# Sums of squares of the dilated heads from a rounded and a remaining part, in a large one-core transformer kernel

## The reference, cut to what matters

```python
qkv = (h @ w_in).reshape(bsz, seq, A_N_GROUPS, 3, A_HEADS, A_HEAD_DIM)   # 3 groups, q/k/v, 16 heads of 64
for g, (window, dilation) in enumerate(A_GROUPS):
    q = rope(rms_norm(qkv[:, :, g, 0], q_gain[g]), positions)
    k = rope(rms_norm(qkv[:, :, g, 1], k_gain[g]), positions)
    v = qkv[:, :, g, 2]
    o, lse = dilated_window_attention(q, k, v, window, dilation)
# rms_norm: x * rsqrt(mean(x*x over the 64 of a head) + 1e-6) * gain
```

## Time and profile before

| | us |
|---|---|
| median of 3 runs | 3809.71 (3798.45 to 3812.93) |
| the profiled execution, its own time | 3802.57 |
| its span | 3800.8 |
| dilated stage, first stretch (from 1966 to 2101 us) | 135 |
| dilated stage, second stretch (2101 to 2640 us) | 539 |
| TensorE busy over the span | 3484.3 (92%) |
| VectorE, ScalarE, GpSimd busy | 1575.9, 1416.8, 1190.1 |

### The profile page before, as it was taken

One profiled execution on the slowest core, in us unless ns is written; L12 is line 12 of the kernel. 1 busy time (PEld: TensorE's weight loads), 2 busy tenths in 40 slices (PEclk: granted clock), 3 DMA queues, 4 the chain that ended last, 5 costly groups with the idle time before them and its releaser, 6 DMA issues.

```text
span 3800.8 us, 43950 instructions
## 1 busy us (share of the span) xinstructions
PE 3484.3 (92%) x17208; PEld 2664.7 (70%) x17208; DVE 1575.9 (41%) x2226; ACT 1416.8 (37%) x1742; POOL 1190.1 (31%) x555
## 2 busy tenths in 40 slices
PE   7999897799959999999638999999899999899999
PEld 4975586578736667666427777777688887678887
DVE  4136525630166666666542332333432132443212
ACT  4225432252235555555133344433432223243221
POOL 2410022634302333333024333322144443334443
PEclk9999998999979999999769999999999999999999
DMA  5322110012227999999623222222032221013222
GB/s 214 102 70 80 66 67 23 1 67 99 89 103 265 348 347 354 366 366 356 268 70 98 69 68 72 73 62 95 23 110 92 99 89 67 23 67 110 93 97 78
DMA packets 94477, 494.51 MB, mean 130 GB/s; under 512 B 21646, under 2 KB 21902, under 8 KB 43760
## 3 DMA queue, kind: packets, MB, share of 16 engines
q1 hardware_dynamic: 74496, 452.75, 33.5%
q0 software_dynamic: 19824, 39.54, 2.9%
HBM read 470.18 MB, written 40.89 MB: 134 GB/s over the span
## 4 chain that ended last, share of the span: by engine, by line
PE 44%; DVE 2%; ACT 2%; issue 1%; POOL 1%; POOLq 0%; DMA 0%; ACTq 0%; DVEq 0%
PE ps L272 10%; PE ps L274 10%; PE ps L273 10%; PE ps L2219 2%; PE ps L2196 2%; PE ps L2174 1%; PE ps L2186 1%; PE ps L2207 1%; PE ps L2175 1%; PE ps L2176 1%; PE ps L2198 1%; PE ps L2848 0%; PE ps L280 0%; PE ps L279 0%; PE ps L278 0%
## 5 line engine op out<-in xcount | busy, mean ns | idle before, releaser
L272 PE MATMUL ps<-arena_r,arena_r 128*128 128x512 f32 x2080 | 842.6, 405 | 39.8 <-POOL ring_r L263 25.0
L273 PE MATMUL ps<-arena_r,arena_r 128*128 128x512 f32 x2080 | 816.0, 392 | 0.0
L263 POOL TENSOR_TENSOR ring_r<-ring,arena_r 128x2048 fp32r<-128x2048 f32 x100 | 466.1, 4662 | 870.8 <-ACT arena_r L259 870.8
L259 ACT ACTIVATE arena_r<-ring 128x2048 fp32r<-128x2048 f32 x166 | 316.6, 1909 | 562.2 <-PE ps L274 408.2
L272 PEld LDWEIGHTS ps<-arena_r,arena_r 128*128 128x128 f32 x2080 | 394.1, 189 | 144.5 <-issue 52.6
L273 PEld LDWEIGHTS ps<-arena_r,arena_r 128*128 128x128 f32 x2080 | 394.7, 190 | 88.5 <-issue 10.6
L263 POOL TENSOR_TENSOR arena_r<-ring,arena_r 128x2048 fp32r<-128x2048 f32 x66 | 304.2, 4609 | 414.2 <-ACT arena_r L259 414.1
L274 PE MATMUL ps<-arena_r,arena_r 128*128 128x512 f32 x1056 | 410.8, 389 | 0.0
L274 PE MATMUL ps<-arena_r,ring_r 128*128 128x512 f32 x1024 | 404.9, 395 | 0.0
L1949 DVE TENSOR_TENSOR arena_r<-arena,arena_r 128x2048 fp32r<-128x2048 f32 x132 | 301.9, 2288 | 168.5 <-ACT arena_r L1907 168.3
L1907 ACT ACTIVATE arena_r<-arena 128x2048 fp32r<-128x2048 f32 x132 | 250.5, 1910 | 125.9 <-DMA arena<-we_gu 102.6
(11 more groups left out here) (392 smaller groups left out, 6017.8 us busy)
## 6 DMA issues: line engine op xcount, KB each, us to landing
ring<-wstream SPq DMA_DIRECT2D x193, 1024.0 KB, 4.9
arena<-we_gu SPq DMA_DIRECT2D x132, 1024.0 KB, 8.2
arena<-we_down SPq DMA_DIRECT2D x66, 1024.0 KB, 7.5
arena<-ys SPq DMA_DIRECT2D x32, 512.0 KB, 8.5
arena<-arena SPq DMA_DIRECT2D x192, 64.0 KB, 2.0
arena<-arena SPq DMA_DIRECT2D x32, 128.0 KB, 4.5
arena<-x_t SPq DMA_DIRECT2D x1, 2048.0 KB, 15.1
h<-arena SPq DMA_DIRECT2D x1, 2048.0 KB, 6.6
```

The lines of the kernel that those rows point to most:

```text
L259: act.activation(whalf(c, 0), ring[:, c % NSLOT, :], ACT.Copy).then_inc(sem("chunk_hi"), 1)
L263: pool.tensor_tensor(whalf(c, 1), ring[:, c % NSLOT, :], whalf(c, 0).bitcast(F32), ALU.subtract).then_inc(sem("chunk_lo"), 1)
L272: pe.matmul(out, hi, rhs[0], start=start, stop=False)
L273: pe.matmul(out, hi, rhs[1], start=False, stop=False)
```

## The change

The square is made twice by ScalarE: DSQ in float32 as before, and DSQ_HI in the rounded type. VectorE subtracts the two into DSQ_LO (`square_low`, one TENSOR_TENSOR with both inputs in SBUF). The sum is then made by two products of rounded numbers, of a rounded copy of `pair` with DSQ_HI and DSQ_LO. The copy of the raw projection comes after the squares and has two buffers, so that it waits for the norm before last only. The sums stand ahead of the fifth eighth of the next half, no longer behind the first.

```diff
+        DRAWS = (DRAW, view(R + 32768, T))
+        DSQ_HI, DSQ_LO, PAIR = rounded(R + 33792, T), rounded(R + 34304, T), rounded(R + 33280, P)
...
                 def between(eighth):
-                    if eighth == 1 and before is not None:
-                        pair_sums(before, h - 1)
                     if eighth == 2 and aside is not None:
                         aside()
+                    if eighth == 4 and before is not None:
+                        pair_sums(before, h - 1)
...
             def pair_sums(n, h):
-                pe.wait_ge(sem("dil_evac"), h + 1)
+                pe.wait_ge(sem("dil_sq_lo"), n + 1)
                 if n >= 1:
                     pe.wait_ge(sem("dil_ln"), n)
-                pe.matmul(bank(7), C["pair"], DSQ, start=True, stop=True).then_inc(sem("dil_ss"), 1)
+                pe.matmul(bank(7), PAIR, DSQ_HI, start=True, stop=False)
+                pe.matmul(bank(7), PAIR, DSQ_LO, start=False, stop=True).then_inc(sem("dil_ss"), 1)
...
+                    if n >= 2:
+                        act.wait_ge(sem("dil_qn"), n - 1)
                     if n >= 1:
-                        act.wait_ge(sem("dil_qn"), n)
                         act.wait_ge(sem("dil_ss"), n)
-                    act.activation(DRAW, bank(5 + h % 2), ACT.Copy)
-                    act.activation(DSQ, bank(5 + h % 2), ACT.Square).then_inc(sem("dil_evac"), 1)
+                    act.activation(DSQ, bank(5 + h % 2), ACT.Square)
+                    act.activation(DSQ_HI, bank(5 + h % 2), ACT.Square).then_inc(sem("dil_sq"), 1)
+                    act.activation(DRAWS[n % 2], bank(5 + h % 2), ACT.Copy).then_inc(sem("dil_evac"), 1)
...
+            act.activation(PAIR, C["pair"], ACT.Copy)
...
-                dve.scalar_tensor_tensor(DQN, DRAW, v(("a_q_norm", "a_k_norm")[s], g, 1), DRS,
+                dve.scalar_tensor_tensor(DQN, DRAWS[n % 2], v(("a_q_norm", "a_k_norm")[s], g, 1), DRS,
                                          ALU.mult, ALU.mult).then_inc(sem("dil_qn"), 1)
+
+            def square_low(h):
+                n = dil_norm(h)
+                dve.wait_ge(sem("dil_sq"), n + 1)
+                dve.tensor_tensor(DSQ_LO, DSQ, DSQ_HI.bitcast(F32), ALU.subtract).then_inc(sem("dil_sq_lo"), 1)
...
-            def step(h):
+            def step(h, with_square=True):
+                if with_square and dil_norm(h - 1) is not None:
+                    square_low(h - 1)
                 if h >= 2 and dil_norm(h - 2) is not None:
                     rotated(h - 2)
...
             for u in range(LAST):
+                first = dil_share(u)[0]
+                if dil_norm(first - 1) is not None:
+                    square_low(first - 1)
                 masked_max(u)
...
                 for h in dil_share(u):
-                    step(h)
+                    step(h, h != first)
```

More of the change, by code:

```diff
@@ L115 @@
     "ff0_value", "ff0_silu", "ff0_hid_hi", "ff0_hid_lo", "ff0_down", "ff0_down_sum",
-    "ff1_value", "ff1_silu", "ff1_hid_hi", "ff1_hid_lo", "ff1_down", "ff1_down_sum",
+    "ff1_value", "ff1_silu", "ff1_hid_hi", "ff1_hid_lo", "ff1_down", "ff1_down_sum", "dil_sq", "dil_sq_lo",
 )
```

## The result

| | before | changed |
|---|---|---|
| median, 7 runs each | 3809.71 us (3797.44 to 3817.74) | 3783.42 us (3777.85 to 3792.88) |
| profiled execution, own time | 3802.57 | 3779.68 |
| stage: first product to first scores | 141.0 | 131.6 |
| first scores to last product of a half | 543.5 | 527.8 |

The ratio of the changed kernel to the one before is 0.9939, with a 95% interval of 0.9921 to 0.9957. The kernel is faster by 0.6%, 26 us between the medians and 23 us between the two profiled executions.

A forecast was written before the change was run, and what follows sets the result against it. TensorE was taken as the bound, so only time off its stream or waits counts. Savings of 7.5 and 15.2 us gave 3779.9 from the profile, 3787.0 from the median; forecast 3783 us, its own range 3774 to 3792, overall 3762 to 3802.

The forecast's parts named there:

- The sum: Whole kernel: 7.5 and 15.2 us saved in the two stretches, 22.7 us off the profiled 3802.6, giving 3779.9.
- the clock: First stretch: granted clock falls to half three times behind waits, costing 1.7 us each; no change counted, 5 us either way.
- Cost of the split sums, 0.45 us: TensorE: both rounded products of a sum take 0.45 us with no float32 switch; 0.97 if they behave like the old ones.
- Waits behind odd halves, 1.27 us, nine: TensorE ahead of sums: VectorE's subtraction is ready 4.0 us after an odd half, TensorE arrives at 2.73.
- The lock: Behind halves 2, 8, 14: GpSimd's line 263 holds VectorE's two-SBUF-input subtraction; TensorE waits 3.4 us, three times in the first stretch.
- The first rival, no lock on the path: Subtraction precedes line 263 or is not held: three 3.4 us waits go, 3768 us; margin 0.35 us; chance 0.17.
- First stretch, 7.5 us: Stage's first product to first scores: each group of six halves falls from 10.26 to 7.74 us, 2.5 saved three times.
- Second stretch, 15.2 us: First scores to last half: 7.4 us behind even halves, 2.0 behind odd, 0.4 last norm, 5.4 for three norms inside units.
- The transposition stays covered: Second stretch behind held subtractions: probabilities ready at 9.35 us, transposition at 9.95, so the delay is hidden by 0.6 us.
- The slower rival: Lock reaches the transposition in nine units of the second stretch, each 1 us beyond slack costing 9 us; up to 3823; chance 0.07.
- The second raw buffer costs and gives nothing: Raw projection copy: the second buffer costs nothing, since its wait for the norm ended before the half did.
- The price of a float32 sum: TensorE: upper bound of 0.97 us (0.56 + 0.41) for a sum if it behaves like the old float32 ones.

The follow-up runs named there:

- the experiment with PSUM: Changed kernel with the float32 square of the first 18 halves written to an idle PSUM bank instead of SBUF: stretches 119.1 and 527.9 us, total 3767.6.
- With the waits removed: Changed kernel with first-stretch squares in PSUM and ScalarE's chunk rounding moved behind an odd half's evacuation or the unit's exponential: ratio 0.9848 to the kernel before, median 3749.1 us.

## Why the prediction was right

The profiled execution moved from 3802.6 to 3779.7 us. The sum said 22.7 us; it was 22.9. The mechanism was right, step by step; the agreement to 0.2 us was luck. At full clock the edit itself saved 7.2 + 14.0 = 21.2 us, 1.5 less than forecast. Some 4 us more came from the clock, for which the forecast counted no change: the lower level took 15.9 and 13.7 us of the two stretches before, 12.1 and 9.7 us after. And 2.2 us were lost outside the two stretches. By its steps:

- **Cost of the split sums, 0.45 us.** Right where nothing is waited for (0.45, or 0.47 where the next product is counted in). Behind a wait the two products start 0.34 us apart (2021.13, 2021.47), 0.11 more than counted, 12 times.
- **Waits behind odd halves, 1.27 us, nine.** Measured 1.22 behind q and k and 1.07 to 1.08 where a v half follows. Nine, as counted.
- **The lock.** Forecast from 0.95 to 5.5 us after the end of the half, wait 3.4 us. Half 8 ended at 2030.52 - 3.33 - 12 x 0.227 = 2024.5 us; line 263 ran from 0.9 to 5.5 us after it, and TensorE waited 3.33 to 3.36 us three times. That the subtraction's second input in SBUF is the cause, only the experiment with PSUM shows. The page "SBUF — State Buffer" of the Trainium skill, section "Who interferes with whom", has the rule by which a VectorE instruction with a single such input, outside the modes that use both ports, is free of GpSimd. By that rule, the trace agrees (the three that met line 263 took 0.69 us). A single large input is not enough by itself: the scaling of the probabilities (line 2367) has one, and where it started at 2159.55 us, beside a line 263 that ended at 2161.77, it took 2.63 us instead of 0.62. The first rival, no lock on the path, fell for this kernel, though the margin was what it said: 0.40 us for 0.35.
- **First stretch, 7.5 us.** Measured 9.5, but 7.2 by the edit. A group of six halves at full clock took 2060.22 - 2016.66 = 43.56 us before, from one group's first sum to the next group's, and 2014.02 - 1972.86 = 41.16 us after: 2.4 us saved, three times, for 2.5 forecast. The rest is the clock: it fell twice, for 3.4 us each, before the first scores, against three times (the earlier trace rows is one of those), and rose 1.0 us earlier at the stage's start. The two starts not shown so far, before and after:

```profile
2060.22 1.13 PE L2186 MATMUL ps<-arena,cst 128*128 128x512 f32 x2 [0.49 <-ACT arena L2260]
```

```profile
1972.86 0.39 PE L2189 MATMUL ps<-arena_r 128*128 128x512 f32 x1
```

- **Second stretch, 15.2 us.** Measured 15.7, but 14.0 by the edit. At full clock, a unit with the sum of an even half takes 2120.36 - 2109.99 = 10.37 us from transposition to transposition before and 2134.47 - 2124.47 = 10.00 after, one with the sum of an odd half 2130.99 - 2120.36 = 10.63 and 2124.47 - 2113.94 = 10.53:

```profile
2109.99 0.82 PE L2207 MATMUL ps<-cst,arena 128*128 128x128 f32 x6
```

```profile
2113.94 0.82 PE L2211 MATMUL ps<-cst,arena 128*128 128x128 f32 x6
...
2124.47 0.82 PE L2211 MATMUL ps<-cst,arena 128*128 128x128 f32 x6
```

Over all units the even ones are 0.37 or 0.38 us shorter (forecast 0.41), the odd ones 0.10 to 0.13 (0.14), and the three norms within units 1.74 each (1.8). Twelve units without a sum did not change. The other 1.7 us are three units in which the lower clock stood for different times. (Six units hold two halves, not three; the forecast does not use that number.) Behind an odd half the values were released by line 2280:

```profile
2117.47 0.82 ACT L2280 ACTIVATE arena<-ps 128x768 f32<-128x768 f32 x1
```

and the values and a later transposition on TensorE:

```profile
2118.34 1.52 PE L2223 MATMUL ps<-arena 128*64 128x128 f32 x12 [0.51 <-ACT arena L2280]
...
2134.47 0.81 PE L2211 MATMUL ps<-cst,arena 128*128 128x128 f32 x6
```

2117.47 + 0.82 = 2118.29, and the values start at 2118.34. Fourteen waits of 0.54 to 0.57 us, forecast 0.54.

- **The transposition stays covered.** VectorE in that next unit:

```profile
2125.79 4.71 DVE L2343 TENSOR_TENSOR arena_r<-arena,arena_r 128x512 fp32r<-128x512 f32 x1 [1.70 <-ACT arena_r L2265]
2130.43 0.95 DVE L2359 CUSTOM_DVE_ANT_0 ps<-ps,arena 128x768 f32<-128x768 f32 x1
...
2132.70 0.62 DVE L2367 TENSOR_SCALAR arena<-arena,small 128x768 f32<-128x768 f32 x1
```

The subtraction is held until 2130.50, then come the maxima, and the probabilities are ready at 2132.70 + 0.62 = 2133.32. The transposition starts at 2134.47, 1.15 us later; forecast 0.6. The slower rival did not come about: all 14 waits at the transposition lie in the last part of the stage, and the kernel before has as many there.
- **The second raw buffer costs and gives nothing.** Shown, with one buffer in its place.
- **The price of a float32 sum.** This was only a bound (0.97 us); undisturbed it is 0.87.

What the forecast did not say is where the rest of the gain had gone. A split sum saves 0.40 us, 19 us for 48. The lock (10 us), the third operation of ScalarE ahead of the values (7.7 us) and 0.7 us more of wait behind nine odd halves (6 us) give that back, and some 5 us more by this account, so that the later place alone, with the old float32 sum, is worth as much as the full change (0.9929 against 0.9939, intervals that overlap). With the waits removed both parts add up: 0.9848.

That the measured median is within a microsecond of the forecast is luck as well. In the ten traces the stage starts anywhere from 1951 to 1972 us, and its last part takes 74 to 88 us.

## What to carry to other kernels

When a short helper instruction is moved to VectorE, look not at its 0.7 us but at what GpSimd runs at that moment: with two SBUF inputs it may wait for a whole instruction of 4.6 us, and one input in PSUM avoided it here. Price a moved wait by both ends, the new place and the new length of the hand-over; the place paid here, and the cheaper arithmetic only once the hand-over was hidden. And ask what stands ahead of the hand-over on its engine without need: moving a 1.9 us chunk rounding behind it shortened the changed kernel's two stretches by 31.8 us, where the change itself had saved 25.2.

## What the runs showed of the hardware

- Exclusion by order, both ways: a VectorE subtraction that started 0.27 us after GpSimd's took 4.82 us; where it started 0.34 us before, GpSimd's took 5.04 instead of 4.58 us, and the subtraction 0.92 instead of 0.69.
- With one of its two inputs in PSUM the same subtraction took 0.69 us beside a GpSimd instruction that had started 0.38 us before it, three times of three.
- A float32 matmul of 128x512 amid rounded ones holds TensorE for 0.87 us (0.45 for two passes, the rest ahead of the second product behind it); behind a wait 0.97.
- Behind a wait of over 1 us, the next two products of rounded numbers started 0.34 us apart instead of 0.23.
- The last part of the stage (16 units, no edit) took 81.2 and 81.3 us before and after, but 87.9 us with squares in PSUM and 74.3 with the split sums at the old place. The granted clock was at the lower level there for 17.1 us before and after, 30.7 us with the squares in PSUM and 3.4 us with the sums at the old place. Half of these differences, 6.8 us each, is what the times differ by (6.6 and 6.9). What decides how long the lower level lasts there stays open; it was not tested.
